# MLP weights split by accumulating DMAs instead of GpSimd subtractions

## Chip, cores and metric

One core of one Trainium2 chip runs the whole program. The metric is the device time of one execution in microseconds.

## What is computed

A decoder trunk of four layers over 512 tokens of width 1024, all in float32. Each layer is a token mixer (dilated window attention in layers 0 and 3, indexer-selected sparse attention in layer 1, gated DeltaNet in layer 2) and then an MLP:

```python
for i in range(DEPTH):
    h = rms_norm(x, norm_mix[i])
    y = mixer_a / mixer_b / mixer_c (h, ...)          # i mod 3
    x = x + y
    x = x + squared_relu_mlp(rms_norm(x, norm_mlp[i]), mlp_w1[i], mlp_w2[i])

def squared_relu_mlp(h, w1, w2):                      # w1: 1024 x 4096, w2: 4096 x 1024
    return jnp.square(jax.nn.relu(h @ w1)) @ w2
```

## The kernel before

Activations are held transposed: channels on the 128 partitions, 512 tokens along the row. Every product with a weight matrix is made of three fp32r products, which together keep nearly float32 accuracy. A weight w is split into `w_hi` (w rounded to fp32r) and `w_lo = w - w_hi`, an activation likewise into a high and a low part, and TensorE adds w_hi·a_hi, w_hi·a_lo and w_lo·a_hi in one PSUM bank.

The weights come in 202 chunks of 1 MB, in the order of the list `CHUNKS`. A chunk n uses slot n % 2 of three pairs of buffers: `raw` (as loaded), `w_hi` and `w_lo`. Each buffer is 128 partitions by 8 by 256 elements, 8 KB in a partition. Four engines hand a chunk on:

- **SP** loads it into `raw` by one DMA (L509) once `raw` is free, that is once the low part of chunk n-2 has been made (`w_lo_done`, L520 and L579).
- **ACT** rounds it with one copy of 2048 columns into `w_hi` (`rounding`, L777). It waits for the load and for TensorE's last matmul on chunk n-2 (`lin_done`), because that matmul frees `w_hi` and `w_lo` of the slot.
- **POOL** (GpSimd) makes `w_lo = raw - w_hi` in four subtractions of 512 columns (`split`, L620), and raises `w_lo_done` with the last.
- **PE** waits for `w_lo_done` and runs the chunk's matmuls.

An MLP takes 32 chunks, in four quarters of 8: chunks 0 to 3 of a quarter are columns of w1 ("up"), chunks 4 to 7 are columns of w2 ("down"). A chunk has two tiles, j = 0 and 1, of 24 matmuls each (L2004): 8 row blocks c by the three products. In the up half the hidden tile is finished off PE: DVE takes relu from PSUM (L1345), ACT squares it (L847) and rounds it to `g_hi` (L849), and DVE subtracts for `g_lo` (L1348). In the down half DVE adds each tile to the residual x (L1360).

ACT's program order in an up half is: hidden tile 2k, hidden tile 2k+1, then the rounding of chunk k+2. So the rounding comes after the square and copy of the tile that ended chunk k. In a down half ACT has only the roundings. Within a mixer and around it the order of ACT's and POOL's work is written out by hand: `round_ahead(n)` and `split_ahead(n)` stand for chunk n+2 and are called where chunk n ends. Ahead of an MLP ACT also prepares its input (`prepare`, L788: `h_hi`; L793: squares), and TensorE sums these squares in layers 0 and 3 (`square_sum`, L1938) between the last tiles of the output projection (L1957).

The quarters are loops on all engines. The other 74 chunks, of the mixers and their output projections, go the same way through ACT and POOL.

Of the kernel before, what the change touches and what calls it, by code (L numbers as in the profile page):

```python
# [16 lines left out]
F32 = mybir.dt.float32  # L17
# [8 lines left out]
DM = 1024  # L26
# [74 lines left out]
def trunk(nc, x_in, rel_bias, params, c_gates, masks, bucket_rows, bias_mask, mlp_w1, mlp_w2,  # L101
# [4 lines left out]
    for n, c in enumerate(CHUNKS):  # L106
        first_chunk.setdefault(c[:2], n)
        chunk_at[c[:3]] = n
        tile0.append(tile0[n] + {"ao": CT, "bo": 4}.get(c[0], 2))

    stepwise = [n for n, c in enumerate(CHUNKS) if n == 0 or c[0] == "chd" and c[2] == 0]
    raw_value, at = [], [0, 0]
    for n, c in enumerate(CHUNKS):
# [9 lines left out]
    with ExitStack() as ctx:  # L123
# [52 lines left out]

        raw_loaded = [sem(f"raw_loaded{s}") for s in range(2)]
        w_lo_part, w_hi_part = sem("w_lo_part"), sem("w_hi_part")
        w_hi_done, w_lo_done, lin_done = sem("w_hi_done"), sem("w_lo_done"), sem("lin_done")
        par_loaded, com_loaded, bias_in_loaded = sem("par_loaded"), sem("com_loaded"), sem("bias_in_loaded")  # L180
        x_loaded = [sem(f"x_loaded{s}") for s in range(2)]
# [325 lines left out]
        def _(sp):  # L507
# [6 lines left out]
            def chunk(n):  # L514

                stage, i, k, kt, _ = CHUNKS[n]
                r = raw[n % 2]
                wide = r.rearrange("p k n -> p (k n)").rearrange("p (k n) -> p k n", n=DM)
                if n >= 2:
                    sp.wait_ge(w_lo_done, n - 1)  # L520
                quad = r.rearrange("p k n -> p (k n)").rearrange("p (k n) -> p k n", n=TOK)
                if stage == "av":
                    g, half = divmod(k, 2)
                    load(n, quad, rows(a_w_in[i // 3], 3072 + TOK * g, TOK, 4, TOK * half))
                elif stage == "aqk":
                    f, g = divmod(k, 3)
                    for s in range(2):
                        load(n, r[:, :, P * s:P * s + P], rows(a_w_in[i // 3], 1536 * s + 512 * g + P * f, P))
                elif stage == "ao":
                    load(n, wide, rows(a_w_out[i // 3], 0, DM, 2, 2 * P * k))  # L530
                elif stage == "bo":
                    z, c0 = k // 2, TOK * (k % 2)
                    for s in range(2):
                        r0 = (8 * z + 4 * s) * HD
                        src = b_w_out[0][r0:r0 + 4 * HD, c0:c0 + TOK].rearrange("(t p) n -> p t n", p=HD)
                        load(n, quad[HD * s:HD * s + HD, :, :], src)
                elif stage == "out":
                    load(n, r[:], rows(c_w_out[0], k * CW, CW))
                elif stage == "cab":
                    w = c_w_in[0]  # L540
                    load(n, r[:, :, 0:8], rows(w, 4096, 8))
                    load(n, r[:, :, 8:GATE_A], rows(w, 0, GATE_A - 8))
                    load(n, r[:, :, GATE_A:GATE_A + 8], rows(w, 4104, 8))
                    load(n, r[:, :, GATE_A + 8:CW], rows(w, 0, CW - GATE_A - 8))
                elif stage == "chd":
                    for s in range(2):
                        load(n, r[:, :, P * s:P * s + P], rows(c_w_in[0], DM * (2 * (k % 2) + s) + P * (k // 2), P))
                elif stage == "bkw":
                    w = b_w_in[0]
                    for s in range(2):  # L550
                        load(n, r[:, :, HD * s:HD * s + HD], rows(w, 2048, HD))
                    load(n, r[:, :, P:P + 8], rows(w, 2112, 8))
                    load(n, r[:, :, P + 8:CW], rows(w, 0, P - 8))
                elif stage == "bqi":
                    load(n, r[:], rows(b_w_in[0], 1536 + k * CW, CW))
                elif stage == "bv":
                    load(n, r[:], rows(b_w_in[0], 1280, CW))
                elif stage == "bk":
                    load(n, r[:], rows(b_w_in[0], 1024, CW))
                elif stage == "bq":  # L560

                    for t in range(2):
                        a = 8 * (k // 2) + 2 * (k % 2) + t
                        for s in range(2):
                            c = P * t + HD * s
                            load(n, r[:, :, c:c + HD], rows(b_w_in[0], (a + 4 * s) * HD, HD))

            def mlp_chunks(i, n0, q):

                c_up = [sp.snap(q * DM + k * CW) for k in range(4)]  # L570
                r_down = c_up[0]
                free = [sp.snap(q * 8 + (n0 + k - 1)) for k in range(8)]
# [34 lines left out]

        @block.gpsimd
        def _(pool):
            def split(n, value=None, lo=0, hi=CT):  # L610

                value = n + 1 if value is None else value
                if n:
                    pool.wait_ge(w_hi_done, value)
                s = n % 2
                for c in range(lo, hi, 2):
                    k = slice(c, c + 2)
# [127 lines left out]
            for li, i in enumerate(layers):  # L745
# [11 lines left out]
                    for k in range(4):  # L757
                        split_ahead(first_chunk["out", i] + k)
                n = first_chunk["mlp", i]
                with pool.Fori(0, QUARTERS - 1) as q:  # L760
                    for k in range(8):
                        split(n + k, q * 8 + (n + k + 3))
                for k in range(8):
                    split_ahead(n + 8 * (QUARTERS - 1) + k)


        @block.scalar
        def _(act):
            def rounding(n, raw_v=None, lin_v=None):

                s = n % 2
                raw_v = raw_value[n] if raw_v is None else raw_v
# [78 lines left out]
            def mlp(li, i, m):  # L851
                n = first_chunk["mlp", i]
                T, G, X = tile0[n], 8 * QUARTERS * li, added(li, True)
                with act.Fori(0, QUARTERS - 1) as q:
# [2 lines left out]

                    def ahead(k):
                        v = act.snap(q * 64 + raw_value[n + k + 2])
                        rounding(n + k + 2, v, t0[2 * k + 2])  # L860

                    for k in range(4):
                        for j in (2 * k, 2 * k + 1):
# [1005 lines left out]
        def _(pe):  # L1869
            def product(n, t, acts, kt, lo, hi, act_sem, act0, tok, own_bank=None):  # L1870
# [25 lines left out]
                in_steps = n in stepwise and j == 0  # L1896
                if lo == 0:
                    if not in_steps:
                        pe.wait_ge(w_lo_done, n + 1)
                    if own_bank is None and t >= 2 and evac[t - 2][0] is not None:  # L1900
                        pe.wait_ge(*evac[t - 2])
                for k in range(lo, hi):
# [3 lines left out]
                    if in_steps and k % 6 == 0:  # L1906
                        if c + 2 < CT:
                            pe.wait_ge(w_lo_part, 3 * stepwise.index(n) + c // 2 + 1)
                        else:
                            pe.wait_ge(w_lo_done, n + 1)  # L1910
# [30 lines left out]
            def joined(i, j, pairs, lo, hi):  # L1941
# [2 lines left out]
                last = pairs[-1] == A_PAIRS - 1  # L1944
                t = tile0[n0 + last] + j
                if lo == 0:
                    pe.wait_ge(w_lo_done, n0 + 1)
                    pe.wait_ge(*evac[t - 2])
                for k in range(lo, hi):
                    f, z = pairs[k // 3], k % 3  # L1950
                    if f >= 2 and z == 0:
                        pe.wait_ge(w_lo_done, n0 + 2)
# [96 lines left out]
            def mlp(li, i):  # L2049
# [4 lines left out]
                def norm_beside(t):  # L2054
                    if t == 0:
                        mlp_norm(li, i)

                mlp_quarter(n, 8 * (2 * li + 1), [n + k + 1 for k in range(8)], {k: X + k for k in range(-1, 7)}, v_g, v_g,
                            norm_beside)
                looped = QUARTERS - (li + 1 == len(layers))  # L2060
                with pe.Fori(1, looped) as q:
                    v_lo = [pe.snap(q * 8 + (n + k + 1)) for k in range(8)]
                    v_x = {k: pe.snap(q * 8 + (X + k)) for k in range(-1, 7)}
                    v_g = {k: pe.snap(q * 8 + (G + k)) for k in range(1, 9)}
                    mlp_quarter(n, 8 * (2 * li + 1), v_lo, v_x, v_g, v_g)
                for q in range(looped, QUARTERS):
                    v_g = {k: q * 8 + G + k for k in range(1, 9)}
                    mlp_quarter(n, 8 * (2 * li + 1), [q * 8 + n + k + 1 for k in range(8)],
                                {k: q * 8 + X + k for k in range(-1, 7)}, v_g, v_g, out_beside)

            spread, summed = [0], [0]
# [17 lines left out]
            def mixer_a(li, i):  # L2089
# [15 lines left out]
                def values(g):  # L2105
# [3 lines left out]
                    for half in range(2):  # L2109
# [4 lines left out]
                        pe.wait_ge(w_lo_done, n + 1)  # L2114
# [548 lines left out]
```

## Time and profile before

| | |
|---|---|
| time, median of 3 runs | 2774.07 us (2773.97 to 2775.56) |
| the profiled execution | 2774.79 us; its span in the trace 2773.0 us |
| PE busy | 2708.8 us, 98% of the span |
| POOL busy | 1362.4 us, 49% |
| ACT busy | 1086.8 us, 39% |
| DVE busy | 1051.7 us, 38% |
| DMA | 227.87 MB, mean 82 GB/s |

Each engine works through its own queue; what one engine waits for is given by semaphores. A busy time is the sum over the engine's instructions. The chain that ended last is followed back from the last instruction; an engine's time on it is time in which nothing else could have ended the program sooner.

### The profile page before, as it was taken

What the parts mean: (1) busy time and instruction counts of PE and PEld (TensorE: products, weight loads), DVE (VectorE), ACT (ScalarE), POOL (GpSimd) and SP (SyncE); (2) the same over time, 40 slices, a digit from 0 to 9 for tenths busy, and PEclk for the clock granted to TensorE, in tenths of its full rate; (3) what the DMA queues carried; (4) which work ended last, traced back from release to release, by engine and by line L of the source; (5) the groups of instructions that cost most, each with busy time, mean ns of one, the idle gap of its engine ahead of it and who ended that gap; (6) DMA issues with size and microseconds to landing.
All of it is one profiled execution on the core that took longest, in us unless ns stands there. A gap on an engine that the chain in (4) does not pass through costs nothing.

```text
span 2773.0 us, 37296 instructions
## 1 busy us (share of the span) xinstructions
PE 2708.8 (98%) x14594; PEld 2186.7 (79%) x14594; DVE 1051.7 (38%) x1966; ACT 1086.8 (39%) x1649; POOL 1362.4 (49%) x1042
## 2 busy tenths in 40 slices
PE   8999999999989999999899999999999999999999
PEld 6977688888756788888788887888888977688887
DVE  4044622113486522113777874311123044622112
ACT  5355633223446433223334344322234355533222
POOL 4577354445446345445544442445455576345443
PEclk9999999999999999999999999999999999999999
DMA  4322122323422132233312110232323322122232
GB/s 143 99 69 64 51 92 91 106 91 92 106 46 70 54 107 91 91 106 91 85 47 55 38 62 22 92 101 91 106 91 98 100 54 69 55 98 91 93 105 76
DMA packets 273440, 227.87 MB, mean 82 GB/s; under 512 B 29221, under 2 KB 260389, under 8 KB 273301
## 3 DMA queue, kind: packets, MB, share of 16 engines
q1 hardware_dynamic: 262578, 216.66, 25.9%
q10 hardware_dynamic: 10722, 9.28, 1.5%
q8 instruction: 96, 1.57, 0.2%
q14 instruction: 44, 0.35, 0.0%
HBM read 223.62 MB, written 2.30 MB: 81 GB/s over the span
## 4 chain that ended last, share of the span: by engine, by line
PE 91%; DVE 4%; ACT 2%; POOL 1%; issue 1%; DMA 1%; ACTq 0%; SPq 0%; DVEq 0%; POOLq 0%
PE bank L2004 50%; PE bank L1911 20%; PE bank L2127 5%; PE bank L2367 2%; PE bank L2507 2%; PE bank L2087 1%; PE bank L2184 1%; PE bank L2200 1%; PE bank L1957 1%; POOL w_lo L620 1%; PE bank L2164 1%; PE bank L2157 1%; PE bank L2294 1%; PE bank L2214 1%; PE bank L1938 1%
## 5 line engine op out<-in xcount | busy, mean ns | idle before, releaser
L620 POOL TENSOR_TENSOR w_lo<-raw,w_hi 128x512 fp32r<-128x512 f32 x808 | 1082.2, 1369 | 1086.8 <-ACT w_hi L777 1067.6
L777 ACT ACTIVATE w_hi<-raw 128x2048 fp32r<-128x2048 f32 x201 | 383.7, 1909 | 461.1 <-PE bank L2004 423.3
L2004 PE MATMUL bank<-h_hi,w_hi 128*128 128x512 f32 x1024 | 400.8, 391 | 0.0
L2004 PE MATMUL bank<-g_hi,w_hi 128*128 128x512 f32 x1024 | 398.6, 389 | 0.0
L2004 PE MATMUL bank<-h_hi,w_lo 128*128 128x512 f32 x1024 | 398.4, 389 | 0.0
L2004 PE MATMUL bank<-g_hi,w_lo 128*128 128x512 f32 x1024 | 398.4, 389 | 0.0
L2004 PE MATMUL bank<-h_lo,w_hi 128*128 128x512 f32 x1024 | 398.4, 389 | 0.0
L2004 PE MATMUL bank<-g_lo,w_hi 128*128 128x512 f32 x1024 | 398.4, 389 | 0.0
L1911 PE MATMUL bank<-h_hi,w_hi 128*128 128x512 f32 x776 | 316.0, 407 | 4.1 <-POOL w_lo L620 2.9
L1911 PE MATMUL bank<-h_lo,w_hi 128*128 128x512 f32 x776 | 308.8, 398 | 0.0
L1911 PE MATMUL bank<-h_hi,w_lo 128*128 128x512 f32 x776 | 306.7, 395 | 0.0
L847 ACT ACTIVATE arena<-arena 128x512 f32<-128x512 f32 x128 | 80.9, 632 | 425.9 <-DVE arena L1345 425.9
L1345 DVE SCALAR_TENSOR_TENSOR arena<-bank,rs 128x512 f32<-128x512 f32 x128 | 88.6, 692 | 372.6 <-PE bank L2004 349.1
L1360 DVE TENSOR_TENSOR x<-x,bank 128x512 f32<-128x512 f32 x96 | 66.0, 688 | 431.5 <-PE bank L2004 431.5
L2004 PEld LDWEIGHTS bank<-h_hi,w_hi 128*128 128x128 f32 x1024 | 192.3, 188 | 41.3 <-issue 1.4
L2004 PEld LDWEIGHTS bank<-h_lo,w_hi 128*128 128x128 f32 x1024 | 192.3, 188 | 41.0 <-issue 1.4
L2004 PEld LDWEIGHTS bank<-g_hi,w_hi 128*128 128x128 f32 x1024 | 192.3, 188 | 40.0
L2004 PEld LDWEIGHTS bank<-h_hi,w_lo 128*128 128x128 f32 x1024 | 192.3, 188 | 39.8
L2004 PEld LDWEIGHTS bank<-g_lo,w_hi 128*128 128x128 f32 x1024 | 192.3, 188 | 39.7
L2004 PEld LDWEIGHTS bank<-g_hi,w_lo 128*128 128x128 f32 x1024 | 192.3, 188 | 39.7
L1911 PEld LDWEIGHTS bank<-h_hi,w_hi 128*128 128x128 f32 x776 | 146.7, 189 | 42.0 <-issue 11.8
L1911 PEld LDWEIGHTS bank<-h_lo,w_hi 128*128 128x128 f32 x776 | 146.6, 189 | 34.9 <-issue 6.9
(276 smaller groups left out, 3801.1 us busy)
## 6 DMA issues: line engine op xcount, KB each, us to landing
raw<-in_mlp_w SPq DMA_DIRECT2D x128, 1024.0 KB, 5.3
raw<-in_a_w_in SPq DMA_DIRECT2D x48, 512.0 KB, 5.2
raw<-in_c_w_in SPq DMA_DIRECT2D x32, 512.0 KB, 5.5
raw<-in_a_w_in SPq DMA_DIRECT2D x12, 1024.0 KB, 5.1
raw<-in_b_w_in SPq DMA_DIRECT2D x18, 256.0 KB, 3.9
raw<-in_a_w_out SPq DMA_DIRECT2D x4, 1024.0 KB, 5.0
raw<-in_b_w_in SPq DMA_DIRECT2D x4, 1024.0 KB, 5.4
arena<-bias_scratch ACTq DMA_DIRECT2D x16, 256.0 KB, 3.6
```

The lines of the kernel that those rows point to most:

```text
L620: ins = nc.gpsimd.tensor_tensor(w_lo[s][:, k, :], raw[s][:, k, :], w_hi[s][:, k, :].bitcast(F32), ALU.subtract)
L777: nc.scalar.activation(w_hi[s][:], raw[s][:], ACT.Copy).then_inc(w_hi_done, 1)
L847: nc.scalar.activation(gsq[j % 2], relu_t[j % 2], ACT.Square).then_inc(gsq_done, 1)
L1345: nc.vector.scalar_tensor_tensor(relu_t[j % 2], lin_bank[j % 2][:], 0.0, rs, ALU.max, ALU.mult).then_inc(relu_done, 1)
L1360: nc.vector.tensor_tensor(x[:, c, :], x[:, c, :], lin_bank[c % 2][:], ALU.add).then_inc(x_added, 1)
L1911: mm = nc.tensor.matmul(o, lhsT, rhs, start=start, stop=stop)
L1938: mm = nc.tensor.matmul(stat_bank[:], ones, sq[c % 2], start=c == 0, stop=c == CT - 1)
L1957: mm = nc.tensor.matmul(lin_bank[t % 2][:], w[(n0 + f // 2) % 2][:].rearrange("p k n -> p (k n)")[:, c:c + P], a[:, f, :], start=k == 0, s ...
L2004: mm = nc.tensor.matmul(lin_bank[j][:], w[s][:, c, P * j:P * j + P], a[:, c, :], start=c + z == 0, stop=c == CT - 1 and z == 2)
L2127: mm = nc.tensor.matmul(bank[2 + b][:], keys, quads[w][:, c, :], start=half + c + z == 0, stop=half == 1 and c == 3 and z == 2)
L2367: mm = nc.tensor.matmul(out[z:z + HD], lhsT[:, z:z + HD], rhs, start=start, stop=stop)
L2507: mm = nc.tensor.matmul(bk4(3)[:, c, :], atl[k % 3][:, c, :], Tm[:, c, :], start=True, stop=True)
```

## The change

Only the 128 MLP chunks are changed. POOL computes nothing for them any more.

- **ACT** rounds a chunk in two halves of 1024 columns (row blocks 0 to 3 and 4 to 7), each raising `w_high`. It then waits for each and writes the negative of the rounded half into `w_lo` (a copy with scale -1), raising `w_neg`. That is four activations of 1024 columns in place of one of 2048.
- **POOL** waits for `w_neg` of a half and issues an accumulating DMA of 512 KB from `raw` onto `w_lo`: w_lo = -w_hi + raw. Each half has its own semaphore, `w_added`. POOL's loop over the quarters is written out.
- **PE** waits for the first half ahead of row block 0 of tile 0 and for the second ahead of row block 4, where it waited once for the chunk.
- **SP** waits for both halves of chunk n-2 before it loads chunk n. The first quarter of each MLP is written out, the other three stay a loop.

`w_lo_done` now counts the mixers' chunks alone (`low_count`), and waits on it are renumbered.

```diff
+    def added_value(li, m):
+        return 16 * (4 * QUARTERS * li + m // 2 + 1)
...
-                if n >= 2:
-                    sp.wait_ge(w_lo_done, n - 1)
+                if n >= 2 and CHUNKS[n - 2][0] == "mlp":
+                    for half in range(2):
+                        sp.wait_ge(w_added[n % 2][half], added_value(*of_mlp(n - 2)))
+                elif n >= 2:
+                    sp.wait_ge(w_lo_done, low_count[n - 2])
...
-                    sp.wait_ge(w_lo_done, free[k])
+                    if first and k < 2:
+                        sp.wait_ge(w_lo_done, low_count[n0 + k - 2])
+                    else:
+                        for half in range(2):
+                            sp.wait_ge(w_added[(n0 + k) % 2][half], free[k] if first else sp.snap(free[k]))
...
-                with sp.Fori(0, QUARTERS) as q:
+                mlp_chunks(i, n_mlp, 0)
+                with sp.Fori(1, QUARTERS) as q:
...
+            def add_raw(s, ready):
+                for half in range(2):
+                    k = slice(4 * half, 4 * half + 4)
+                    pool.wait_ge(w_neg, ready[half])
+                    pool.dma_start(w_lo[s][:, k, :].bitcast(F32), raw[s][:, k, :], accum_op=ALU.add).then_inc(w_added[s][half], 16)
...
+                if CHUNKS[n][0] == "mlp":
+                    v = high_value(*of_mlp(n))
+                    add_raw(n % 2, (v + 1, v + 2))
+                    return
...
-                with pool.Fori(0, QUARTERS - 1) as q:
-                    for k in range(8):
-                        split(n + k, q * 8 + (n + k + 3))
-                for k in range(8):
-                    split_ahead(n + 8 * (QUARTERS - 1) + k)
+                for k in range(8 * QUARTERS):
+                    split_ahead(n + k)
...
-                nc.scalar.activation(w_hi[s][:], raw[s][:], ACT.Copy).then_inc(w_hi_done, 1)
+                if not of_layer:
+                    nc.scalar.activation(w_hi[s][:], raw[s][:], ACT.Copy).then_inc(w_hi_done, 1)
+                    return
+                parts = [slice(4 * half, 4 * half + 4) for half in range(2)]
+                for k in parts:
+                    nc.scalar.activation(w_hi[s][:, k, :], raw[s][:, k, :], ACT.Copy).then_inc(w_high, 1)
+                for k, v in zip(parts, high_v):
+                    act.wait_ge(w_high, v)
+                    nc.scalar.activation(w_lo[s][:, k, :], w_hi[s][:, k, :].bitcast(F32), ACT.Copy,
+                                         scale=-1.0).then_inc(w_neg, 1)
...
-                        if j == 0:
-                            pe.wait_ge(w_lo_done, v_lo[k])
...
+                            if j == 0 and c % 4 == 0:
+                                pe.wait_ge(w_added[s][c // 4], v_lo[k])
```

## Rows read from the trace of the kernel before

**Rows 1.** The page: engines' busy time (share, instructions), and the chain by line.
```profile
PE 2708.8 (98%) x14594; PEld 2186.7 (79%) x14594; DVE 1051.7 (38%) x1966; ACT 1086.8 (39%) x1649; POOL 1362.4 (49%) x1042
PE bank L2004 50%; PE bank L1911 20%; PE bank L2127 5%; PE bank L2367 2%; PE bank L2507 2%; PE bank L2087 1%; PE bank L2184 1%; PE bank L2200 1%; PE bank L1957 1%; POOL w_lo L620 1%; PE bank L2164 1%; PE bank L2157 1%; PE bank L2294 1%; PE bank L2214 1%; PE bank L1938 1%
```

**Rows 2.** The chain, start us and length, over the whole span: first and fourth MLP.
```profile
349.75 342.77 PE bank L2004 x1512
2421.88 326.46 PE bank L2004 x1440
```

**Rows 3.** Groups of instructions: count | busy us, mean ns | idle before, releaser.
```profile
L620 POOL TENSOR_TENSOR w_lo<-raw,w_hi 128x512 fp32r<-128x512 f32 x808 | 1082.2, 1369 | 1086.8 <-ACT w_hi L777 1067.6
L777 ACT ACTIVATE w_hi<-raw 128x2048 fp32r<-128x2048 f32 x201 | 383.7, 1909 | 461.1 <-PE bank L2004 423.3
L849 ACT ACTIVATE g_hi<-arena 128x512 fp32r<-128x512 f32 x128 | 80.9, 632 | 4.0
```

**Rows 4.** Timeline (start us, us, [idle before]) of a chunk in an up half.
```profile
431.24 0.39 PE L2004 MATMUL bank<-h_hi,w_hi 128*128 128x512 f32 x1
442.12 0.39 PE L2004 MATMUL bank<-h_hi,w_hi 128*128 128x512 f32 x1
...
444.24 1.90 ACT L777 ACTIVATE w_hi<-raw 128x2048 fp32r<-128x2048 f32 x1
446.23 5.50 POOL L620 TENSOR_TENSOR w_lo<-raw,w_hi 128x512 fp32r<-128x512 f32 x4 [7.76 <-ACT w_hi L777]
448.48 0.63 ACT L847 ACTIVATE arena<-arena 128x512 f32<-128x512 f32 x1 [2.33 <-DVE arena L1345]
```

**Rows 5.** Timeline: a rounding in a down half.
```profile
431.44 1.92 ACT L777 ACTIVATE w_hi<-raw 128x2048 fp32r<-128x2048 f32 x1 [8.96 <-PE bank L2004]
```

**Rows 6.** DMA issues of the whole span: count, KB each, median us to landing.
```profile
raw<-in_mlp_w SPq DMA_DIRECT2D x128, 1024.0 KB, 5.3
arena<-bias_scratch ACTq DMA_DIRECT2D x32, 64.0 KB, 3.8
out_y<-arena SPq DMA_DIRECT2D x2, 512.0 KB, 3.3
out_y<-arena SPq DMA_DIRECT2D x4, 256.0 KB, 2.3
```

**Rows 7.** Busy time by stretch; the last three columns are clock, DMA share, GB/s.
```profile
440.00:442.00 2.00, 2.00 (x11) 1.65 (x10) 0.00 (x0) 0.00 (x0) 0.00 (x0) 1.00 0.93 285
442.00:444.00 2.00, 2.00 (x11) 1.65 (x10) 0.69 (x1) 0.93 (x2) 0.00 (x0) 1.00 0.59 206
```

**Rows 8.** Timeline ahead of layer 0's MLP.
```profile
329.50 1.91 ACT L777 ACTIVATE w_hi<-raw 128x2048 fp32r<-128x2048 f32 x1
332.15 0.72 ACT L788 ACTIVATE h_hi<-x,par 128x512 fp32r<-128x512 f32 x1 [0.74 <-DVE x L1328]
...
333.45 1.12 PE L1938 MATMUL bank<-sq,com 128*128 128x512 f32 x2 [0.29 <-ACT sq L793]
...
341.55 1.02 PE L1938 MATMUL bank<-sq,com 128*128 128x512 f32 x2
```

**Rows 9.** The same place: low parts of x on DVE, beside POOL's subtractions and after them.
```profile
331.49 5.92 POOL L620 TENSOR_TENSOR w_lo<-raw,w_hi 128x512 fp32r<-128x512 f32 x4 [26.54 <-ACT w_hi L777]
332.98 1.59 DVE L1316 SCALAR_TENSOR_TENSOR h_lo<-x,par,h_hi 128x512 fp32r<-128x512 f32 x1 [0.18 <-ACT h_hi L788]
338.48 0.74 DVE L1316 SCALAR_TENSOR_TENSOR h_lo<-x,par,h_hi 128x512 fp32r<-128x512 f32 x1
```

**Rows 10.** Timeline ahead of layer 1's and layer 2's MLP: rounding of their first chunk.
```profile
951.17 1.90 ACT L777 ACTIVATE w_hi<-raw 128x2048 fp32r<-128x2048 f32 x1
1737.28 1.90 ACT L777 ACTIVATE w_hi<-raw 128x2048 fp32r<-128x2048 f32 x1
```

**Rows 11.** The chain: start of the same two MLPs on PE.
```profile
960.14 5.45 PE bank L2004 x24
1746.25 5.45 PE bank L2004 x24
```

More of the change, by code:

```diff
@@ L109, in trunk, with high_value, of_mlp @@
         tile0.append(tile0[n] + {"ao": CT, "bo": 4}.get(c[0], 2))
+    low_count, count = [], 0
+    for c in CHUNKS:
+        count += c[0] != "mlp"
+        low_count.append(count)
+    def added_value(li, m):
+        return 16 * (4 * QUARTERS * li + m // 2 + 1)
+    def high_value(li, m):
+        return 2 * (8 * QUARTERS * li + m)
+    def of_mlp(n):
+        return list(layers).index(CHUNKS[n][1]), CHUNKS[n][2]
     stepwise = [n for n, c in enumerate(CHUNKS) if n == 0 or c[0] == "chd" and c[2] == 0]
@@ L178, in trunk @@
         w_lo_part, w_hi_part = sem("w_lo_part"), sem("w_hi_part")
+        w_high, w_neg = sem("w_high"), sem("w_neg")
+        w_added = [[sem(f"w_added{s}{half}") for half in range(2)] for s in range(2)]
         w_hi_done, w_lo_done, lin_done = sem("w_hi_done"), sem("w_lo_done"), sem("lin_done")
@@ L568, in mlp_chunks @@
             def mlp_chunks(i, n0, q):
-                c_up = [sp.snap(q * DM + k * CW) for k in range(4)]
+                li = list(layers).index(i)
+                first = isinstance(q, int)
+                c_up = [q * DM + k * CW if first else sp.snap(q * DM + k * CW) for k in range(4)]
                 r_down = c_up[0]
-                free = [sp.snap(q * 8 + (n0 + k - 1)) for k in range(8)]
+                free = [q * 64 + added_value(li, k - 2) for k in range(8)]
                 for k in range(8):
@@ L609, in _, with split @@
         def _(pool):
-            def split(n, value=None, lo=0, hi=CT):
-                value = n + 1 if value is None else value
+            def add_raw(s, ready):
[3 more added lines that the diff above has]
+                    pool.dma_start(w_lo[s][:, k, :].bitcast(F32), raw[s][:, k, :], accum_op=ALU.add).then_inc(w_added[s][half], 16)
+            def split(n, lo=0, hi=CT):
+                if CHUNKS[n][0] == "mlp":
+                    v = high_value(*of_mlp(n))
+                    add_raw(n % 2, (v + 1, v + 2))
+                    return
                 if n:
-                    pool.wait_ge(w_hi_done, value)
+                    pool.wait_ge(w_hi_done, low_count[n])
                 s = n % 2
@@ L759, in _, with rounding @@
                 n = first_chunk["mlp", i]
-                with pool.Fori(0, QUARTERS - 1) as q:
-                    for k in range(8):
-                        split(n + k, q * 8 + (n + k + 3))
-                for k in range(8):
-                    split_ahead(n + 8 * (QUARTERS - 1) + k)
+                for k in range(8 * QUARTERS):
+                    split_ahead(n + k)
         @block.scalar
         def _(act):
-            def rounding(n, raw_v=None, lin_v=None):
+            def rounding(n, raw_v=None, lin_v=None, high_v=None):
                 s = n % 2
+                of_layer = CHUNKS[n][0] == "mlp"
+                if of_layer and high_v is None:
+                    high_v = [high_value(*of_mlp(n)) + half + 1 for half in range(2)]
                 raw_v = raw_value[n] if raw_v is None else raw_v
@@ L859, in ahead @@
                         v = act.snap(q * 64 + raw_value[n + k + 2])
-                        rounding(n + k + 2, v, t0[2 * k + 2])
+                        high = high_value(li, k + 2)
+                        rounding(n + k + 2, v, t0[2 * k + 2], [act.snap(q * 16 + (high + half + 1)) for half in range(2)])
                     for k in range(4):
@@ L1898, in product @@
                     if not in_steps:
-                        pe.wait_ge(w_lo_done, n + 1)
+                        pe.wait_ge(w_lo_done, low_count[n])
                     if own_bank is None and t >= 2 and evac[t - 2][0] is not None:
@@ L1909, in product @@
                         else:
-                            pe.wait_ge(w_lo_done, n + 1)
+                            pe.wait_ge(w_lo_done, low_count[n])
                     mm = nc.tensor.matmul(o, lhsT, rhs, start=start, stop=stop)
@@ L1946, in joined @@
                 if lo == 0:
-                    pe.wait_ge(w_lo_done, n0 + 1)
+                    pe.wait_ge(w_lo_done, low_count[n0])
                     pe.wait_ge(*evac[t - 2])
@@ L1951, in joined @@
                     if f >= 2 and z == 0:
-                        pe.wait_ge(w_lo_done, n0 + 2)
+                        pe.wait_ge(w_lo_done, low_count[n0 + 1])
                     w, a = ((w_hi, g_hi), (w_hi, g_lo), (w_lo, g_hi))[z]
@@ L2056, in norm_beside @@
                         mlp_norm(li, i)
-                mlp_quarter(n, 8 * (2 * li + 1), [n + k + 1 for k in range(8)], {k: X + k for k in range(-1, 7)}, v_g, v_g,
+                mlp_quarter(n, 8 * (2 * li + 1), [added_value(li, k) for k in range(8)], {k: X + k for k in range(-1, 7)}, v_g, v_g,
                             norm_beside)
@@ L2061, in mlp @@
                 with pe.Fori(1, looped) as q:
-                    v_lo = [pe.snap(q * 8 + (n + k + 1)) for k in range(8)]
+                    v_lo = [pe.snap(q * 64 + added_value(li, k)) for k in range(8)]
                     v_x = {k: pe.snap(q * 8 + (X + k)) for k in range(-1, 7)}
@@ L2067, in mlp @@
                     v_g = {k: q * 8 + G + k for k in range(1, 9)}
-                    mlp_quarter(n, 8 * (2 * li + 1), [q * 8 + n + k + 1 for k in range(8)],
+                    mlp_quarter(n, 8 * (2 * li + 1), [added_value(li, 8 * q + k) for k in range(8)],
                                 {k: q * 8 + X + k for k in range(-1, 7)}, v_g, v_g, out_beside)
@@ L2113, in values @@
                         late_sum = li == 0 and g == 0 and half == 0
-                        pe.wait_ge(w_lo_done, n + 1)
+                        pe.wait_ge(w_lo_done, low_count[n])
                         s = n % 2
```

## The prediction

> **What bounds the kernel now.** I read the page's busy times first: PE is busy for 98% of the span, POOL for 49%, ACT for 39%; the chain by line puts half of the span on the MLP's matmuls at L2004, and POOL's subtractions at L620 have 1% of it [rows 1]. The chain in order of time says more: each MLP is one unbroken piece, in the first layer 342.77 us for 1512 matmuls, in the last 326.46 us for 1440 [rows 2]. That is 226.7 ns a matmul in both, 10.88 us for a chunk of 48. The clock there is 1.00 [rows 7]. So no chunk of an MLP is waited for today, and what the change takes from POOL (512 of 808 subtractions of 1369 ns, 701 us of busy time [rows 3]) is off the path. It can't make an MLP shorter. What it can do is make a low part late, so the question is the slack of that hand-over.
>
> **The hand-over today.** In an up half a chunk starts on PE at 431.24 and the next at 442.12; the third is due at 453.00 [rows 4]. The slot of chunk 0 is free at 442.12. DVE and ACT finish the last hidden tile first, so the rounding starts at 444.24, 2.12 us after the slot is free; POOL subtracts from 446.23 to 451.73, 1.27 us before the due time [rows 4]. In a down half the rounding starts at 431.44, 0.20 us after the slot is free [rows 5], so there is 1.9 us more.
>
> **ACT's part.** One copy of 2048 columns (1909 ns) becomes four of 1024. A copy of 512 takes 632 ns [rows 3], so on a straight line one of 1024 takes 632 + (1909 - 632)/3 = 1058 ns. I count no overlap of successive copies. The first negative half is there 3 x 1.06 = 3.17 us after the rounding starts, the second after 4.23 us. The waits between them are for work already done, except some hundredths. ACT gets 128 x 2.32 = 297 us more to do, and is at 50% of the span. In an up half it ends at 444.24 + 4.23 = 448.47, and the next square is ready for it at 448.48 [rows 4]: the cover is just enough. If it were gone, nothing would stop yet, since a hidden tile is needed only in the down half, and its PSUM bank is freed by DVE.
>
> **POOL's and the DMA's part.** The add of the first half has from 444.24 + 3.17 = 447.41 to 453.00, **5.59 us**, for issue, transfer and completion. The second half is needed at row block 4, 12 matmuls or 2.72 us later, at 455.72. With an overhead V, and a transfer time X for 512 KB, the two run one behind the other: V + X must be under 5.59 and V + 2X under 455.72 - 447.41 = **8.31 us**. In a down half the limits are 7.5 and 10.2 us. No accumulating DMA, and none from POOL, is in the trace, so both terms are bounded.
> X: a 1 MB load moves in about 2 x 0.93 + 2 x 0.59 = 3.04 us of full use [rows 7], 1.5 us for 512 KB. Stores out of SBUF give 3.3 - 2.3 = 1.0 us for 256 KB more, so 2.0 us for 512 KB [rows 6]. An add also has to read its destination. If that read hides beside the rest, X is 1.5; if each byte read counts, 3.0; if the adding itself is slow, more, and no row has an upper end. I take 2.4, between the first two and near the store's row, since a load or store is bound by one side only.
> V: a load takes 5.3 us to land, so 2.3 us beside its transfer; 64 KB on ACT's queue take 3.8; 512 KB out take 3.3, so 1.3 [rows 6]. Bounds 1.3 and 3.8; I take 2.5, nearest to the load, the only one of these that writes the same kind of buffer. Then V + X = 4.9 (limit 5.59) and V + 2X = 7.3 (limit 8.31). **No stall, 0.7 and 1.0 us to spare.**
>
> The trace shows the MLP's loads taking 3 us of DMA time in 10.88. With two adds, 3.0 + 4.8 = 7.8 us are taken. The load of a slot is now issued when its adds have landed: by these values 7.3 us after 447.41, at 454.7, with data until about 458. The next chunk's adds start at 458.3, so load and add just miss each other. A load has 442.12 + 21.76 + 2.1, that is some 11 us of slack, so the later issue costs nothing.
>
> Here a rule of the Trainium skill bears on the sum, against the change. Rows 7 price only a plain transfer. "Collectives: The Full Stack" (section on the bandwidth ceiling) says that the add inside a DMA is free, but that it has two source reads on one ring, and gives a ratio of 1.93 between copying and reducing. By it an estimate of X is 1.93 x 1.52 = 2.9 us and V + 2X = 8.4, just over the limit. No row of this case shows it.
>
> **PE's waits.** Two waits for one per chunk. Tiles 0 of chunks 0 and 4 have a wait for each of their 8 row blocks now, and the piece of 1512 matmuls is unbroken over them [rows 2]: nothing.
>
> **SP and POOL queues.** SP's written-out quarter and POOL's written-out loop add instructions to fetch, on engines with nothing due. POOL's two waits per chunk stand in the order of chunks, and nothing is queued behind them in an MLP; at a mixer's start the next POOL work needs results that come after the last MLP chunk was rounded.
>
> **The stretch ahead of an MLP.** In layer 0 the first MLP chunk is rounded at 329.50, ahead of `h_hi` (332.15) and the first square; PE waits for the first square and sums it at 333.45, and is busy from there on [rows 8]. With 4.23 us for the rounding ACT is free at 333.73, not 332.15: **+1.58 us**, which PE doesn't get back. Against it stands that POOL's subtractions (331.49 to 337.41) are gone; beside them DVE took 1.59 us for a low part of x, after them 0.74 [rows 9]. From there PE takes (341.55 - 333.45)/5 = 1.62 us a tile [rows 8]; DVE's slow low parts can have set that pace in two tiles at most, and I count 0 to 0.3 us as given back. Net +1.3 to +1.6. Layer 3 repeats it. Layers 1 and 2 round their first MLP chunk at 951.17 and 1737.28 [rows 10] and need it at 960.14 and 1746.25 [rows 11]: less 3.17 us, both leave 5.80 us for V + X = 4.9, and ACT's next work waits for DVE or PE. Nothing.
>
> **The sum.** 2 x 1.3 = +2.6 us, at the most +3.2. The profiled execution took 2774.79 us (2773.0 of them the span), 0.7 above the median; on it the sum is 2777.4 to 2778.0, and on the median, which I predict, 2774.07 + 2.9 = **2777.0 us**.
>
> **Price of a late add.** Let the limit be passed by d in an up half. Of two successive chunks the first waits d; the second has had its own slot work shifted only once and finds its data there. Four chunks of each quarter (2 to 5) hang on an up-half rounding, so 2 waits per quarter, 32 in all: 32 d.
>
> **Rivals.**
> - *The reads double, slight stall.* X = 3.0 and V = 2.5 give 8.5 against 8.31: 32 x 0.2 = 6 us. With V = 3.8 it is 9.8, d = 1.5, 48 us. For it: an add must read twice the bytes. Against it: reads and writes may not share one limit. The rule above belongs here; its 8.4 gives +3. Taken in the middle, V = 3: d = 0.7, 22 us, so about 2799; from 2780 to 2825.
> - *The add is slow, and the DMA engines become the bound.* Slower from the point where 2X + 3.0 passes 10.88, X above 3.9. At three times the plain transfer, X = 4.5 to 4.7, a chunk takes 12.2 us, 1.4 more, on 128 chunks 180 us: about 2955. From X = 3.5 to 6 it goes from 2825 to over 3200. For it: nothing bounds X from above in the trace. Against it: the DMA engines have 70% of their time free (3.04 of 10.88 us are taken), and rows of 4 KB in a partition are long.
> - *Faster.* POOL's subtractions no longer slow DVE where DVE sets the pace ahead of an MLP. 1.59 against 0.74 us for a low part [rows 9], some 1.7 us at each of four places, gives -7 and with ACT's delay hidden 2767. Against it: there PE is continuous in the chain.
> - *The change does not do what it says*: POOL would still subtract in the MLP. Then 2774. The count at L620 decides; I give it no chance of its own.
>
> **How the numbers follow.** No stall 0.52; slight stall 0.22; slow adds 0.21; faster 0.05. About 0.2% (5.5 us) is what a measurement can tell from no change. Faster by more: 0.05. Within: the first case, 0.52, as the slight stall starts beyond it. Slower: 0.43. The likeliest case's own range is 2773 to 2780. For 8 in 10 the range must take in the slight stall whole and the lower part of the slow adds: 2771 to 2880, which leaves out half of the faster case and some 0.16 of the slow adds.
>
> **What would show it.** L620 at 296 subtractions, POOL busy near 660 us; w_hi in MLP chunks at 1.06 us for 1024 columns; ACT near 1385 us. The MLPs still as unbroken pieces of 342.8 us in the chain, if the forecast holds; DMA time of an MLP up from 3.0 to 7.8 us per chunk. The step from L777 to L788 ahead of layers 0 and 3 longer by 1.6 us. The forecast is wrong if PE at L2004 waits for `w_lo`: waits at every second chunk of the up halves mean the slight stall, waits in down halves too mean that X is above 3.7.

## The result and the profile after

The changed kernel takes 2781.57 us (median of 11 runs, 2777.92 to 2786.82); the kernel before, run beside it, 2774.65 us. The ratio is 1.0024, 95% interval 1.0016 to 1.0031: slower by 6.9 us at the medians. That is in the range (2771 to 2880), near its lower end, but the likeliest case (no stall, 2777.0, "within 0.2%") is missed by a little; the interval lies on both sides of 0.2%. The time is in the range because the range takes in stalls: it falls at the lower edge of the slight stall (from 2780), whose sign, a wait at every second chunk of the up halves, is not what the trace shows.

The page of the changed kernel, in the same sections as before: busy times, two DMA queues (each with its packets, MB and share of 16 engines), groups (count | busy us, mean ns | idle before, releaser), a DMA issue with its landing.

```profile
span 2778.0 us, 37519 instructions
PE 2712.7 (98%) x14594; PEld 2189.1 (79%) x14594; DVE 1035.6 (37%) x1966; ACT 1340.2 (48%) x2033; POOL 907.8 (33%) x786
q1 hardware_dynamic: 262578, 216.66, 25.9%
q0 software_dynamic: 36864, 134.23, 25.1%
L644 POOL DMA_DIRECT2D w_lo<-raw x256 | 222.9, 873 | 1227.0 <-ACT w_lo L824 1216.0
L659 POOL TENSOR_TENSOR w_lo<-raw,w_hi 128x512 fp32r<-128x512 f32 x296 | 404.9, 1393 | 315.9 <-ACT w_hi L817 296.4
L821 ACT ACTIVATE w_hi<-raw 128x1024 fp32r<-128x1024 f32 x256 | 255.7, 1046 | 324.2 <-PE bank L2053 324.2
L824 ACT ACTIVATE w_lo<-w_hi 128x1024 fp32r<-128x1024 f32 x256 | 254.8, 1043 | 0.0
w_lo<-raw POOLq DMA_DIRECT2D x256, 512.0 KB, 6.2
```

The change is made as described: 296 subtractions are left of 808 [rows 3], POOL issues 256 adds of 0.87 us each, ACT has 253 us more to do than before [rows 1]. POOL's busy time was forecast near 660 us and is 907.8: the issuing of the adds (222.9 us) counts as busy time of POOL, and the forecast had nothing for it. POOL is not on the path in the MLPs, so this costs nothing. The MLP's matmuls have moved to L2053. The chain in order of time (start, us, what) shows where they are no longer unbroken. Its long pieces in the four MLPs, with the adds on the chain:

```profile
351.24 342.90 PE bank L2053 x1512
968.20 321.03 PE bank L2053 x1416
1294.43 6.07 DMA w_lo<-raw
1300.63 11.16 PE bank L2053 x48
1754.60 81.63 PE bank L2053 x360
1839.56 8.15 DMA w_lo<-raw
1847.84 250.50 PE bank L2053 x1104
2426.07 92.70 PE bank L2053 x408
2524.97 7.75 DMA w_lo<-raw
2532.76 220.63 PE bank L2053 x972
```

Against rows 2: the first MLP is whole (342.90 for 342.77), the other three wait once each for an add. Measured from the first to the last of their matmuls, the four MLPs take 0.1, 0.9, 1.0 and 0.9 us more, together 2.9. The mixer stretches before them take 1.5, 0.1, -0.6 and 1.1 more, together 2.2. Sum 5.1, where the two spans differ by 5.0 (2778.0 and 2773.0).

The wait at 1300 us is at the last chunk of layer 1's MLP. There ACT doesn't have the roundings alone: the input of the next mixer (`h_hi`, squares) stands ahead of the last roundings.

```profile
1290.61 0.62 ACT L841 ACTIVATE sq<-x 128x512 f32<-128x512 f32 x1
1291.13 1.99 ACT L821 ACTIVATE w_hi<-raw 128x1024 fp32r<-128x1024 f32 x2
1294.43 1.80 POOL L644 DMA_DIRECT2D w_lo<-raw  x2 [8.97 <-ACT w_lo L824]
```

The slot is free at 1289.06 and the chunk is due 10.88 us later, at 1299.94. The first add, issued at 1294.43, has 5.51 us and not the 7.5 of a down half; it takes 6.07.

The time from issue to landing of all 256 adds (min, median, max):

```profile
DMA to landing us min/median/max: 4.6/6.2/9.7
```

### The profile page after: what moved, and what is told of

Same layout as the page of the kernel before. It is cut to its first block, busy times and chain, and to the rows that moved or that the text cites. A ratio compares the mean times of both kernels' runs of the same rounds, so it can differ in the third digit from the quotient of the medians.

```text
span 2778.0 us, 37519 instructions
## 1 busy us (share of the span) xinstructions
PE 2712.7 (98%) x14594; PEld 2189.1 (79%) x14594; DVE 1035.6 (37%) x1966; ACT 1340.2 (48%) x2033; POOL 907.8 (33%) x786
## 4 chain that ended last, share of the span: by engine, by line
PE 89%; DVE 3%; ACT 3%; POOL 2%; DMA 1%; issue 1%; SPq 0%; DVEq 0%; ACTq 0%; POOLq 0%
PE bank L2053 49%; PE bank L1960 20%; PE bank L2176 4%; PE bank L2556 2%; PE bank L2416 2%; PE bank L2136 1%; POOL w_lo L659 1%; PE bank L2233 1%; PE bank L2249 1%; PE bank L2006 1%; DMA w_lo<-raw 1%; PE bank L2213 1%; PE bank L2206 1%; PE bank L2343 1%; PE bank L2263 1%
## 5 line engine op out<-in xcount | busy, mean ns | idle before, releaser
L644 POOL DMA_DIRECT2D w_lo<-raw x256 | 222.9, 873 | 1227.0 <-ACT w_lo L824 1216.0
L659 POOL TENSOR_TENSOR w_lo<-raw,w_hi 128x512 fp32r<-128x512 f32 x296 | 404.9, 1393 | 315.9 <-ACT w_hi L817 296.4
L821 ACT ACTIVATE w_hi<-raw 128x1024 fp32r<-128x1024 f32 x256 | 255.7, 1046 | 324.2 <-PE bank L2053 324.2
L2053 PE MATMUL bank<-h_hi,w_hi 128*128 128x512 f32 x1024 | 401.2, 392 | 0.9 <-DMA w_lo<-raw 0.8
L2053 PE MATMUL bank<-g_hi,w_hi 128*128 128x512 f32 x1024 | 398.9, 390 | 0.5 <-DMA w_lo<-raw 0.5
L2053 PE MATMUL bank<-g_lo,w_hi 128*128 128x512 f32 x1024 | 398.5, 389 | 0.0
L2053 PE MATMUL bank<-g_hi,w_lo 128*128 128x512 f32 x1024 | 398.5, 389 | 0.0
L2053 PE MATMUL bank<-h_lo,w_hi 128*128 128x512 f32 x1024 | 398.5, 389 | 0.0
L2053 PE MATMUL bank<-h_hi,w_lo 128*128 128x512 f32 x1024 | 398.5, 389 | 0.0
L824 ACT ACTIVATE w_lo<-w_hi 128x1024 fp32r<-128x1024 f32 x256 | 254.8, 1043 | 0.0
L2053 PEld LDWEIGHTS bank<-h_hi,w_hi 128*128 128x128 f32 x1024 | 192.2, 188 | 43.3 <-issue 2.3
L2053 PEld LDWEIGHTS bank<-g_hi,w_hi 128*128 128x128 f32 x1024 | 192.2, 188 | 41.4 <-issue 1.6
L2053 PEld LDWEIGHTS bank<-h_lo,w_hi 128*128 128x128 f32 x1024 | 192.2, 188 | 41.0 <-issue 1.4
L2053 PEld LDWEIGHTS bank<-h_hi,w_lo 128*128 128x128 f32 x1024 | 192.2, 188 | 40.0
L2053 PEld LDWEIGHTS bank<-g_lo,w_hi 128*128 128x128 f32 x1024 | 192.2, 188 | 39.8
L2053 PEld LDWEIGHTS bank<-g_hi,w_lo 128*128 128x128 f32 x1024 | 192.2, 188 | 39.8
```

The lines of the kernel that those rows point to most:

```text
L644: pool.dma_start(w_lo[s][:, k, :].bitcast(F32), raw[s][:, k, :], accum_op=ALU.add).then_inc(w_added[s][half], 16)
L659: ins = nc.gpsimd.tensor_tensor(w_lo[s][:, k, :], raw[s][:, k, :], w_hi[s][:, k, :].bitcast(F32), ALU.subtract)
L821: nc.scalar.activation(w_hi[s][:, k, :], raw[s][:, k, :], ACT.Copy).then_inc(w_high, 1)
L824: nc.scalar.activation(w_lo[s][:, k, :], w_hi[s][:, k, :].bitcast(F32), ACT.Copy, scale=-1.0).then_inc(w_neg, 1)
L2053: mm = nc.tensor.matmul(lin_bank[j][:], w[s][:, c, P * j:P * j + P], a[:, c, :], start=c + z == 0, stop=c == CT - 1 and z == 2)
```

## The experiments

Theory A: the loss has two parts, the longer rounding ahead of layers 0 and 3, and adds that now and then land too late. Theory B: the adds are fine; ACT's four activations and PE's second wait cost it all.

**The changed kernel again.**

> The changed kernel once more, as the yardstick for the three others of this call. Both theories: +4 to +9 us on the kernel before. Theory A (rounding delay ahead of layers 0 and 3, plus adds that now and then land late): some MLP chunks are waited for, 0.5 to 1.5 us each, and at other chunks than in the first profile; the start of the layer-0 MLP stands 1.2 to 1.6 us later. Theory B (ACT's longer rounding and PE's second wait cost it all): no PE wait on a w_lo DMA is needed, and the loss is spread over the matmuls.

Measured: 2781.7 us, ratio 1.0026 (1.0017 to 1.0036). The MLPs take 0.3, 0.7, 0.6 and 0.8 us more than before. The adds that PE waits for are again three. The first and the last of them are those of the first profile; the second is another:

```profile
1296.12 5.92 DMA w_lo<-raw
1865.21 5.78 DMA w_lo<-raw
2526.43 7.69 DMA w_lo<-raw
```

**ACT's part alone.**

```diff
-                    pool.dma_start(w_lo[s][:, k, :].bitcast(F32), raw[s][:, k, :], accum_op=ALU.add).then_inc(w_added[s][half], 16)
+                    for c in range(4 * half, 4 * half + 4, 2):
+                        ins = nc.gpsimd.tensor_tensor(w_lo[s][:, c:c + 2, :], raw[s][:, c:c + 2, :],
+                                                      w_hi[s][:, c:c + 2, :].bitcast(F32), ALU.subtract)
+                    ins.then_inc(w_added[s][half], 1)
```

> ACT's four activations and the half-wise waits of the change are kept, but POOL makes w_lo by its subtractions again, two per half after the half's negative, and overwrites it; no accumulating DMA. The first half is ready 3.17 + 2.75 = 5.9 us after the rounding starts (limit 8.76), the second at 8.7 (limit 11.5), so no chunk is late. Theory A: only the delay ahead of layers 0 and 3 is left, +2.5 to +3.2 us, 2777 to 2778, and the MLPs are unbroken. Theory B: the full loss of the change, +6 to +7 us.

Measured: 2776.73 us, 1.0008 (0.9999 to 1.0017). The four MLPs are unbroken and as long as before to 0.1 us; the last:

```profile
2421.59 326.46 PE bank L2056 x1440
```

Theory B falls: with all of ACT's work and PE's waits, but without the DMAs, 1.3 us of 6.3 are left at the medians, and no MLP is longer. That is less than Theory A's 2.5 to 3.2, though the interval reaches 4.7. The trace shows A's longer rounding at both of its places, +1.1 and +1.0 in the stretches ahead of layers 0 and 3, and against them a layer-2 mixer that is 2.8 us shorter, of which more below.

**Another order on ACT.**

```diff
-                for k in parts:
-                    nc.scalar.activation(w_hi[s][:, k, :], raw[s][:, k, :], ACT.Copy).then_inc(w_high, 1)
                 for k, v in zip(parts, high_v):
+                    nc.scalar.activation(w_hi[s][:, k, :], raw[s][:, k, :], ACT.Copy).then_inc(w_high, 1)
                     act.wait_ge(w_high, v)
```

> The changed kernel with ACT's order high 0, negative 0, high 1, negative 1 in place of high 0, high 1, negative 0, negative 1. The first add is issued 1.06 us earlier, and the second has the queue to itself sooner. Theory A: no or fewer late chunks in the trace; of the loss only the delay ahead of layers 0 and 3 stays, +2.5 to +3.5 us. Theory B: unchanged against the changed kernel, +6 to +7 us.

Measured: 2778.04 us, 1.0014 (1.0005 to 1.0023). The median landing is 5.3 us for 6.2; the likely reason is that the second add no longer queues behind the first. No add is on the chain: the MLPs take 0.1, 0.0, 0.0 and 0.0 us more. What is left is in the stretches ahead of layers 0 and 3 (+3.0 and +1.5). Of the 3.0, 1.8 lie before the first MLP chunk is rounded (at 331.29 us, for 329.50 before the change), where no edit touches the kernel; this part differs from run to run.

**The first MLP chunk of layers 0 and 3 back to POOL.** The edit makes these two chunks count as the mixers' do, and counts the values of the waits anew; its core:

```diff
+    def by_pool(c):
+        return c[0] == "mlp" and c[2] == 0 and KINDS[c[1]] == 0
...
-                if CHUNKS[n][0] == "mlp":
+                if CHUNKS[n][0] == "mlp" and not by_pool(CHUNKS[n]):
...
-                of_layer = CHUNKS[n][0] == "mlp"
+                of_layer = CHUNKS[n][0] == "mlp" and not by_pool(CHUNKS[n])
```

> The changed kernel, but the first MLP chunk of layers 0 and 3 is rounded by one copy of 2048 columns and its low part subtracted by POOL, as before. Theory A: the layer-0 MLP starts where it does in the kernel before, and 2.5 to 3.2 us of the loss are gone, +3.5 to +4.5 us remain from late adds. Theory B: nothing gained, +6 to +7 us, since only 2 of 128 roundings are changed.

Measured: 2780.03 us, 1.0016 (1.0007 to 1.0025). The stretches ahead of layers 0 and 3 are at -0.3 and +0.1 us of those before; the MLPs, where late adds remain, take 0.5, 1.9, 0.3 and 1.6 us more. Some 1.7 us less than the changed kernel at the medians: less than A's 2.5 to 3.2, and by the times alone not clear of B's nothing, as the two intervals overlap. The traces carry the verdict.

**Both edits.** The order on ACT and the two chunks by POOL, together.

> The changed kernel with both edits: ACT's order high, negative, high, negative, and the first MLP chunk of layers 0 and 3 split as before by one copy and POOL. Theory A (loss = 0.9 us each ahead of layers 0 and 3, plus late adds): both terms gone, within 0.1% of the kernel before, 2774.5 to 2777, MLPs unbroken, the last square sum 18.4 us after the rounding starts. A rival with a third term (the DMA traffic or the written-out loops slow the rest): +2 to +4 us stay.

Measured: 2776.14 us against 2774.89, 1.0008 (0.9999 to 1.0017). The longest add takes 7.8 us, none is on the chain, and each stretch and each MLP is within 0.4 us of before. With both terms mended the change costs nothing that can be told from zero, though the interval leaves room for up to 4.7 us. It doesn't beat the kernel before, and nothing in the traces says that it could.

**Small loads.**

```diff
-                    load(n0 + k, raw[(n0 + k) % 2][:], src)
+                    load(n0 + k, raw[(n0 + k) % 2][:, 0:1, :], src[:, 0:1, :])
```

> The changed kernel with the MLP's loads cut to row block 0 (128 KB in place of 1 MB; the other seven blocks of the raw buffer keep what was there, so the MLPs compute with other weights). Adds, ACT and PE keep their work. If late adds come from a load that shares the DMA engines: no chunk is waited for, the longest landing falls from 8 or 9 us to under 7.3, and the loss falls to the 2 us of the roundings. If the adds vary by themselves: the waits of 0.5 to 1 us per MLP stay.

Measured: 2781.93 us, 1.0025 (1.0016 to 1.0034). My first case is refuted in its main point: the longest landing falls to 7.8 us only, two late adds stay at places where the changed kernel has them, and the time doesn't fall. One of them is on the chain:

```profile
2525.21 0.86 POOL w_lo L644
2526.06 7.68 DMA w_lo<-raw
2533.79 1.43 PE bank L2053 x5
```

The other is at the last chunk of layer 1's MLP, which is 1.05 us longer than before:

```profile
1302.84 0.47 PE L2053 MATMUL bank<-g_hi,w_hi 128*128 128x512 f32 x1 [0.77 <-DVE x L1377]
```

The profile names DVE, which ended last; but PE needs no result of that DVE add here, and in the kernel before it doesn't wait at this place. The chunk's first add is issued at 1296.40 and lands 6.31 us later, at 1302.71. It meets the loads of the next mixer, which this edit leaves at full size.

Beside the pair of adds on the chain, in the ten microseconds from 2524 to 2534, the DMA queues carry (packets, MB, share):

```profile
q0 software_dynamic: 288, 1.05, 55.9%
q8 instruction: 1, 0.02, 0.6%
```

One instruction fetch of some 16 KB takes 0.6% of 16 engines for 10 us, that is 0.96 us of one engine. The end of the pair, from 2532.0 to 2533.5, looks like this:

```profile
q0 software_dynamic: 5, 0.02, 5.6%
```

For the last 1.5 us the adds keep about one engine of 16 busy (6.25%), with five packets. So the pair is late by the lag of one engine. That the fetch caused the lag is argued: its 0.96 us cover two thirds of it, and what the rest is stays open. By count, for all 128 pairs of this kernel: of 103 without a fetch between issue and landing the later half lands after 6.2 us at the median and 6.4 at most, except two (6.6, and 7.8 for the pair at 1296). Of 25 with one, five lie between 7.0 and 7.7, the others between 6.1 and 6.9. So loads are not the only cause. Where they are at full size they are a second one (the down halves, below). No run takes the fetches away.

The trace of this kernel also shows a third effect, ahead of layer 0. PE has to wait for the first square, and after that its clock falls. TensorE rows and the line of the stretch from 334 to 340 us (PE, PEld, DVE, ACT, POOL, granted clock, DMA share, GB/s):

```profile
334.92 1.33 PE L1987 MATMUL bank<-sq,com 128*128 128x512 f32 x2 [1.44 <-ACT sq L841]
335.48 1.19 PE L2006 MATMUL bank<-g_hi,w_hi 128*128 128x512 f32 x1
334.00:340.00 6.00, 5.08 (x11) 2.96 (x12) 3.38 (x6) 4.49 (x8) 1.05 (x2) 0.72 0.93 175
```

In the changed kernel the same wait is 1.42 us and the clock stays at 1.00:

```profile
335.17 1.12 PE L1987 MATMUL bank<-sq,com 128*128 128x512 f32 x2 [1.42 <-ACT sq L841]
334.00:340.00 6.00, 4.83 (x16) 3.00 (x17) 4.71 (x7) 5.32 (x10) 1.30 (x2) 1.00 0.92 175
```

Inside those six microseconds small_load's clock is at 0.50, which is 1.2 GHz, for some three, and its last square sum comes 1.65 us later after the rounding than in the changed kernel (20.92 for 19.27). Before the change this wait is 0.29 us [rows 8].

**One add per chunk.**

```diff
-                for half in range(2):
-                    k = slice(4 * half, 4 * half + 4)
-                    pool.wait_ge(w_neg, ready[half])
-                    pool.dma_start(w_lo[s][:, k, :].bitcast(F32), raw[s][:, k, :], accum_op=ALU.add).then_inc(w_added[s][half], 16)
+                pool.wait_ge(w_neg, ready[1])
+                pool.dma_start(w_lo[s][:].bitcast(F32), raw[s][:], accum_op=ALU.add).then_inc(w_added[s][0], 16)
```

> The changed kernel with one add of 1 MB per chunk after the second negative, and PE's one wait at row block 0. It lands V + 2X = 2.0 + 5.3 = 7.3 us after the second negative at 3.95, so 11.25 us after the rounding starts; due at 8.76 in an up half and 10.68 in a down half. By the price of the prediction (the first of two successive chunks waits): 32 x 2.5 + 32 x 0.6 = about 100 us, 2865 to 2890. If the waits didn't alternate but each chunk waited: about 200 us.

Measured: 2925.53 us in two runs, 1.0542 (1.0523 to 1.0562), that is +151 us, of which 142 are in the MLPs. The forecast was about 100. A stretch of the chain over four pairs of chunks:

```profile
455.92 6.94 DMA w_lo<-raw
462.90 11.19 PE bank L2049 x48
480.21 6.96 DMA w_lo<-raw
487.21 11.19 PE bank L2049 x48
502.63 8.69 DMA w_lo<-raw
511.37 11.19 PE bank L2049 x48
526.77 6.95 DMA w_lo<-raw
533.77 11.20 PE bank L2049 x48
```

The chain goes through one wait in two chunks. Its releases are 24.31, 24.16 and 22.40 us apart, against 21.76 of PE's own work. PE waits at some of the chunks between too, but shorter (0.65 us at 474.72). An add of 1 MB lands 6.95 us after its issue. The 24.31 is the forecast 2.5 us for a wait of an up half. Three things were missing.

First, the first add of a down half (502.63) takes 8.69, as it shares the engines with a load, and costs 2.4 us where I had 0.6; at this place of a quarter the cost goes from 0.7 to 2.5 us where the clock is full. Second, a chunk that PE has waited for is slower by 0.1 us: 11.17 us at the median from its first matmul to the end of its last, 11.05 for one that didn't wait. Third, and the largest: the clock falls. In the four MLPs it stands at 0.50, which is 1.2 GHz, 15 times for some three microseconds, each time beside a PE wait of 1.8 to 3.0 us; eleven other waits of that length are not followed by it. In the kernel before it never falls in an MLP. Such a chunk, and the clock inside it:

```profile
558.12 12.79 PE bank L2049 x48
559.00:563.00 4.00, 4.00 (x12) 3.13 (x11) 0.00 (x0) 2.79 (x3) 0.72 (x1) 0.57 0.77 262
```

It takes 12.79 us where another after a wait takes 11.19. An estimate: 15 times 1.6 us is 24 us of the 42 missing.

**Plain copies** (the adds without the addition, so `w_lo` holds the weight itself).

```diff
-... raw[s][:, k, :], accum_op=ALU.add).then_inc(w_added[s][half], 16)
+... raw[s][:, k, :]).then_inc(w_added[s][half], 16)
```

> The changed kernel with plain copies in place of the adds (the same two DMAs of 512 KB from raw to w_lo, issued by POOL, without the addition, so w_lo holds the weight itself). It prices the addition: if it costs the second read, a copy has X = 1.3 us against 2.6, lands after 3.2 to 3.7 us where an add lands after 4.6 at the least, and the DMA share in an MLP falls from 0.80 to about 0.54. If the addition costs nothing, the landing stays at 4.6 and more.

Measured: 2777.33 us in one run, MLPs unbroken. The landing, and the queues (packets, MB, share of 16 engines) from 360 to 690 us in this kernel; then the adds' queue in the changed kernel over the same time:

```profile
DMA to landing us min/median/max: 2.8/3.2/5.4
q1 hardware_dynamic: 34352, 31.49, 30.3%
q0 software_dynamic: 8640, 31.46, 23.9%
```
```profile
q0 software_dynamic: 8640, 31.46, 49.5%
```

For 60 transfers of 512 KB a copy takes 0.239 x 330 / 60 = 1.31 us of all engines and an add 0.495 x 330 / 60 = 2.72 us: 2.07 times as much for the same bytes moved.

**Adds of half the size.**

```diff
-                    k = slice(4 * half, 4 * half + 4)
+                    k = slice(4 * half, 4 * half + 2)
```

> The changed kernel with adds of two row blocks of each half in place of four (256 KB; the other two keep only the negative, so the products with the low parts are wrong there). ACT's work and its order are the changed kernel's. An add of 512 KB takes 2.7 us of the DMA engines, so these take 1.36 and land 1.3 us earlier. If late adds make up half of the loss: MLPs unbroken, no PE wait on an add, DMA share of the first MLP 0.55, and +2 to +4 us remain (the roundings ahead of layers 0 and 3, and the clock). If ACT's work or PE's extra waits made the loss in the MLPs: +6 to +7 us as in the changed kernel.

Measured: 2776.01 us against 2775.83, 1.0002 (0.9993 to 1.0011). Landing and, from 360 to 690 us, the busy times, clock and DMA share:

```profile
DMA to landing us min/median/max: 3.3/3.8/5.4
360.00:690.00 330.00, 330.00 (x1458) 273.25 (x1457) 68.76 (x101) 162.27 (x193) 53.91 (x62) 1.00 0.58 143
```

ACT, PE's waits and the number of DMAs are those of the changed kernel; only the adds are shorter, no MLP is longer than before, and the loss is gone. So the loss in the MLPs hangs on the adds' length. The time went further than I expected (+2 to +4 us): the stretches ahead of layers 0 and 3 are still longer by 2.5 and 0.8 us (of the 2.5, 1.6 lie before the first MLP chunk is rounded), and the layer-2 mixer is shorter by 2.8 (434.1 us for 436.9). ACT's part alone shows the same 434.1. In both the clock doesn't fall in that mixer; before, it costs 3.4 us there. In all, with the time lost to the lower clock counted as span x (1 - clock), the two profiles lose 11.3 and 11.5 us, the kernel before 12.8 and the changed kernel 16.1, at places in the mixers that no edit touches and that differ from run to run. So some of the last gain is the clock: over all its runs this kernel loses 13.4 us on the mean, the kernel before beside it 15.0.

## Why the prediction was right, and where it was off

**The MLP can't become shorter.** Right: no kernel here has an MLP below 342.7 us in the chain.

**V and X.** Right in the mean. Nothing in rows 6 or 7 shows an add, and I took 2.5 and 2.4 us. Measured: X = 2.72, V = 4.6 - 2.7 = 1.9, so V + X = 4.6 (predicted 4.9) and V + 2X = 7.3 (predicted 7.3, limit 8.31). That the second sum is met exactly is luck: V was too high by 0.6 and X too low by 0.3, and they cancel. My reason for an X below 3.0, that a load or store is bound by one side only, no run shows. Plain copies confirm the upper of my two rows for X, the one in which each byte read counts. The rule of the Trainium skill ("Collectives: The Full Stack", section "The bandwidth ceiling: the fold count and why AG ≠ RS ≠ AR", that a reduce is slower by its second read) agrees in size: 2.07 measured here inside one SBUF, 1.93 on the page for collectives between cores.

**No stall, 1.0 us to spare.** This is the step that failed, by 2.9 us. I set one landing time against the limit, and the landings are spread from 4.6 to 9.7 us. Three things use up the microsecond. Beside an instruction fetch a pair of adds can land up to 1.5 us later; that is one of the two late adds that remain with small loads. At the end of an MLP the limit isn't that of a down half: at the last chunk of layer 1's MLP it is 5.51 us for 7.5, as ACT has the next norm's work there, and every trace with whole adds in ACT's first order waits at this chunk. And the load of the other slot: I wrote that load and add just miss each other, for two roundings 10.88 us apart. Where an up half ends the next rounding comes 2.12 - 0.20 = 1.9 us sooner [rows 4, 5], so there the load meets the adds, in the first three quarters of an MLP. In the changed kernel these pairs of adds land after up to 9.7 us; the wider limit of the down half (7.5 for the first) holds most of them, not that of 1839.56 with 8.15.

**Price of a late add.** For an up half it was right in form and size: the single add per chunk shows the large wait once in two chunks, at 2.6 us for 2.5 where the clock is full. Of the 42 us that the sum lacked, an estimated 24 are the fallen clock, which it had at nothing, and the rest loads that meet the adds of the down halves and 0.1 us for each slower chunk after a wait.

**ACT's part.** 1046 and 1043 ns for 1058. The overlap that I left out is there: `h_hi` comes 3.80 us after the rounding starts, where the forecast had 4.23.

**Ahead of layers 0 and 3.** The right place, too high a price: PE's first square sum comes 1.13 us later than before and the last one 0.9 (19.27 for 18.37 us after the rounding starts, in both layers), where the forecast had 1.3 to 1.6. In all 1.8 for 2.6 to 3.2. Half of the 0.2 between was given back by POOL's leaving DVE alone: with ACT's part alone, where POOL still subtracts, the last sum comes 0.1 us later (19.39). The stretch ahead of layer 0 is longer by 1.5, but 0.6 of that lie before the rounding, at 330.09 for 329.50.

**Layers 1 and 2, PE's second wait, the written-out loops.** Nothing that a time shows, as forecast. Whether the written-out loops bring some of the fetches that delay the adds was not tested.

**The sum.** 1.8 + 2.9 = 4.7 of the 5.0 us between the two profiled spans; the rest is the difference of mixers that vary from run to run by more than that. The medians differ by 6.9. What the 2 us between are stays open: more late adds in the runs without a profile would do it. The clock is no likely reason, as each run's is on record: the changed kernel loses 14.9 and 16.1 us on the mean of its two sets, the kernel before 15.1, 14.4 and 15.0 in its three.

## What to carry to other kernels

Set the slack of a hand-over against the spread of what fills it, not against its median. Here a pair of adds beside an instruction fetch needed up to 1.5 us more than its usual landing, and one that met a load up to 3.5 (9.7 us for 6.2). Ask at which point of the loop two transfers come closest, not how far apart they are on average; and where a long step is cut in pieces, issue what starts the transfer as soon as its own piece is there. Look at the last round of a loop by itself: what is prepared there for the next stage can shorten a limit that holds in all other rounds.

## What the runs showed of the hardware

- An accumulating DMA in SBUF takes 2.07 times the engine time of a plain copy of the same size (2.72 and 1.31 us for 512 KB); beside that it costs 1.9 us to landing, a copy 1.5. Issuing one keeps POOL busy for 0.87 us.
- With small loads, of 25 pairs of such adds with an instruction fetch (8 to 24 KB) beside them, five landed after 7.0 to 7.7 us, where 6.2 is usual; of 103 without one, one did, and that beside loads. That the fetch is the cause was not tested.
- A chunk of 48 matmuls that PE had to wait for took 11.17 us at the median from its first start to its last end, 11.05 without a wait, at the full clock.
- A PE idle time of 1.44 us was followed by some 3 us at half clock in one run; 1.42 us at the same place in another was not. With one add per chunk it happened 15 times in the MLPs, beside waits of 1.8 to 3.0 us; a chunk of 48 matmuls then took 12.79 us for 11.19.
